# Attention of a hybrid encoder layer: four head groups written out, with the next group's queries placed bank by bank

## The reference

```python
q = (rms_norm(q_lat, q_a_norm) @ w_q_b)         # 512 latent -> 16 heads x (128 + 64)
kv = (rms_norm(kv_lat, kv_a_norm) @ w_kv_b)     # 512 latent -> 16 heads x (128 keys + 128 values)
s = (einsum(q_nope, k_nope) + einsum(q_rope, k_rope)) * scale
s = where(mask, s, -inf)                        # chunk-causal: a query sees keys up to its chunk of 64
o = einsum(softmax(s), v)
y_mla = (o * silu(gate)) @ w_o                  # 2048 x 2048
y_lru = (h * silu(gate)) @ w_o                  # 2048 x 2048, h from the recurrence
merged = sigmoid(m_mla) * y_mla + sigmoid(m_lru) * y_lru
```

## Time and profile before

| what | value |
|---|---|
| median of 3 runs | 2043.49 us |
| profiled execution | 2044.64 us, span 2042.8 us |
| PE busy | 1993.4 us, 98% of the span |
| DVE, ACT, POOL busy | 682.3, 716.8, 905.2 us (33%, 35%, 44%) |
| stretch of the attention's heads and projections | 1070 to 1321 us |
| mean granted TensorE clock | 0.996 of full speed |

### The profile page before, as it was taken

The page is one execution under the profiler, slowest core; times in us unless marked ns, Lnnn a source line. Parts: engine busy times, 40 slices in busy tenths (PEclk is TensorE's granted clock), DMA queues, the critical chain, the costliest instruction groups (busy, mean ns, idle before and its releaser), DMA issues.

```text
span 2042.8 us, 25478 instructions
## 1 busy us (share of the span) xinstructions
PE 1993.4 (98%) x9070; PEld 1658.4 (81%) x9070; DVE 682.3 (33%) x943; ACT 716.8 (35%) x1241; POOL 905.2 (44%) x683
## 2 busy tenths in 40 slices
PE   7999999999999999999999999899999999999996
PEld 6888888888888888888888878788888888888885
DVE  4100000000455647363456545781010250111344
ACT  6322232222353434433344444422222222333333
POOL 2444444444454545454452332154444454444452
PEclk9999999999999999999999999999999999999998
DMA  6533333433223323342352421343333343224232
GB/s 246 178 122 104 123 123 105 143 123 110 96 83 117 109 87 118 98 144 83 107 151 84 145 85 59 147 179 127 113 112 123 123 182 107 84 103 187 102 103 103
DMA packets 128688, 247.06 MB, mean 121 GB/s; under 512 B 15053, under 2 KB 40309, under 8 KB 120565
## 3 DMA queue, kind: packets, MB, share of 16 engines
q1 hardware_dynamic: 116688, 185.09, 27.7%
q10 hardware_dynamic: 11941, 61.17, 7.8%
HBM read 214.26 MB, written 29.36 MB: 119 GB/s over the span
## 4 chain that ended last, share of the span: by engine, by line
issue 59%; POOL 38%; POOLq 1%; DVE 1%; PE 0%; ACT 0%; DVEq 0%
POOL wlo L362 38%; POOLq L361 1%; POOLq L358 0%; DVE x L1241 0%; PE ps L1252 0%; DVE x L1214 0%; DVE stage L1213 0%; DVE x L1244 0%; POOLq L362 0%; ACT stage L790 0%; DVEq L126 0%; DVE nrm L827 0%; DVE nrm L832 0%; DVE nrm L833 0%; DVE nrm L828 0%
## 5 line engine op out<-in xcount | busy, mean ns | idle before, releaser
L362 POOL TENSOR_TENSOR wlo<-raw,whi 128x512 fp32r<-128x512 f32 x672 | 903.9, 1348 | 1111.9 <-ACT whi L378 1111.4
L378 ACT ACTIVATE whi<-raw 128x512 fp32r<-128x512 f32 x672 | 422.2, 632 | 1200.4 <-PE ps L1252 1153.1
L1252 PE MATMUL ps<-hhi,whi 128*128 128x512 f32 x1408 | 548.2, 389 | 1.2 <-POOL wlo L362 1.2
L1252 PE MATMUL ps<-hhi,wlo 128*128 128x512 f32 x1408 | 547.7, 389 | 0.0
L1252 PE MATMUL ps<-hlo,whi 128*128 128x512 f32 x1408 | 547.7, 389 | 0.0
L1252 PEld LDWEIGHTS ps<-hhi,whi 128*128 128x128 f32 x1408 | 264.4, 188 | 56.5 <-POOL wlo L362 1.6
L1252 PEld LDWEIGHTS ps<-hlo,whi 128*128 128x128 f32 x1408 | 264.4, 188 | 55.1 <-issue 0.2
L1252 PEld LDWEIGHTS ps<-hhi,wlo 128*128 128x128 f32 x1408 | 264.3, 188 | 54.7
L912 DVE TENSOR_TENSOR stage<-ps,stage 128x512 f32<-128x512 f32 x16 | 11.1, 692 | 412.4 <-ACT stage L475 410.9
L1252 PE MATMUL ps<-lhi,whi 128*128 128x512 f32 x256 | 100.4, 392 | 2.5 <-DVE llo L821 2.5
L1252 PE MATMUL ps<-llo,whi 128*128 128x512 f32 x256 | 100.3, 392 | 0.0
(11 more groups left out here) (253 smaller groups left out, 2420.0 us busy)
## 6 DMA issues: line engine op xcount, KB each, us to landing
raw<-in_w_in SPq DMA_DIRECT2D x88, 1024.0 KB, 5.0
raw<-in_w_o_lru SPq DMA_DIRECT2D x16, 1024.0 KB, 4.9
raw<-in_w_o_mla SPq DMA_DIRECT2D x16, 1024.0 KB, 4.9
raw<-in_w_out SPq DMA_DIRECT2D x16, 1024.0 KB, 5.0
raw<-in_w_ple_gate SPq DMA_DIRECT2D x16, 1024.0 KB, 4.9
sig_scr<-stage ACTq DMA_DIRECT2D x8, 1024.0 KB, 7.0
raw<-in_w_kv_b SPq DMA_DIRECT2D x32, 256.0 KB, 4.0
stage<-sig_scr ACTq DMA_DIRECT2D x8, 1024.0 KB, 4.8
```

The lines of the kernel that those rows point to most:

```text
L362: pool.tensor_tensor(wlo[:, k % RING], raw[:, k // RAWC, k % RAWC], whi[:, k % RING].bitcast(F32), ALU.subtract).then_inc(lo_ready, 1)
L378: act.activation(whi[:, c % RING], raw[:, c // RAWC % 2, c % RAWC], ACT.Copy).then_inc(hi_ready, 1)
L1252: return pe.matmul(o, l, r, start=start, stop=stop)
```

## The change

The loops over pairs of groups go on PE, ACT and DVE; the four groups are written out. In a group:

- Values are projected by token tiles (banks): tiles 0 and 1 for all four chunks, then tile 2, then the scores 3 and 2 of head 0, then tile 3 (12 matmuls), then the scores 1 and 0. A semaphore `v_done` counts tiles, so ACT and DVE take each from PSUM by itself.
- At the group's end stand the query chunks of the next group, or, in the last group, the first four chunks of the output projection of the recurrence's branch: bank 3 for all four chunks ahead of `values(2)`, bank 2 between the turns of head 3, banks 1 and 0 after them, then `values(3)`.
- ACT splits these four chunks into `whi` after the exps of heads 1, 2 and 3 (one, one, two).
- The next group's keys start with banks 0 to 2 of the first chunk ahead of the claim of the set.
- In the last group DVE splits `llo` tiles 0 to 3 inside heads 1 and 2, two in each; the others follow the attention.

```diff
+            def next_chunk(g, k, ms):
+                c = C_ATT + 3 * KL * (g + 1) + k
+                if ms == (3,):
+                    pe.wait_ge(lo_ready, c + 1)
+                for m in ms:
+                    hi, lo, kn = ahead(g, k, m)      # queries, or lhi/llo after wait_ge(l_split, k + 1)
+                    ...
+                if ms[-1] == 0:
+                    ins.then_inc(chunk_used, 1)
...
+                for m in range(3):
+                    keys(m)
+                if g:
+                    take(ks)
+                keys(3).then_inc(chunk_used, 1)
...
+                for k in range(KL):
+                    new_values(k, 0)
+                    new_values(k, 1)
+                for k in range(KL):
+                    new_values(k, 2)
+                take(ks)
+                pe.wait_ge(kr_lo, 2)
+                pe.wait_ge(qr_lo, g + 1)
+                scores(0, 3)
+                scores(0, 2)
+                for k in range(KL):
+                    new_values(k, 3).then_inc(chunk_used, 1)
+                scores(0, 1)
+                scores(0, 0)
+                for h in range(1, 4):
+                    scores(h, 3)
+                    scores(h, 2)
+                    if h > 1:
+                        values(h - 2)
+                    if h == 1:
+                        take(pt)
+                    for q in (3, 2, 1, 0):
+                        turn(h - 1, q)
+                    scores(h, 1)
+                    scores(h, 0)
+                pe.wait_ge(exp_done, 16 * g + 13)
+                for k in range(KL):
+                    next_chunk(g, k, (3,))
+                values(2)
+                turn(3, 3)
+                turn(3, 2)
+                pe.wait_ge(exp_done, 16 * g + 14)
+                for k in range(KL):
+                    next_chunk(g, k, (2,))
+                turn(3, 1)
+                turn(3, 0)
+                take(ks)
+                for k in range(KL):
+                    next_chunk(g, k, (1, 0))
+                values(3)
```

ACT, in a group's heads:

```diff
+                    if h < 4:
+                        exp(h, 2)
+                        exp(h, 1)
+                        exp(h, 0)
+                        split(c + 2 * KL + RING + h - 1)
+                    if h == 3:
+                        split(c + 2 * KL + RING + 3)
+                        act.wait_ge(exp_done, 16 * g + 16)
+                        act.sem_inc(released[ks], 1)
+                for k in range(KL):
+                    split(c + 3 * KL + RING + k)
```

DVE, in the heads:

```diff
+                        maximum(g, h, 1)
+                        maximum(g, h, 0)
+                    if h < 3 and g == NG - 1:
+                        split_merge(lhi, llo, l_split, 2 * h - 2)
+                        split_merge(lhi, llo, l_split, 2 * h - 1)
```

More of the change, by code:

```diff
@@ L647, in _ @@
             merge_gate_out(1, 0, U_M3, stage_idle)
[L649 to L723, removed]
@@ L728, in _ @@
                 act.dma_start(olo[:, 4 * g:4 * g + 4].bitcast(F32), o_scr[g]).then_inc(o_landed[g], 16)
-            with act.Fori(0, NG) as i:
-                for g in range(2):
+            merge_gate_back(0, 0)
+            for k in range(6, KD):
+                split(C_Y + RING + k)
+            with act.Fori(0, NG - 1) as i:
+                for g in (1, 2):
                     for k in range(KD):
@@ L733, in _ @@
                         if k == 2:
-                            act.wait_ge(y_out, i * 2 + (g + 1))
-                            act.dma_start(stage[:], sig_scr[bass.ds(i + (1 - g) * NG, 1)].rearrange("a q m n -> q (a m) n")).then_inc(sig_landed, 16)
+                            merge_gate_back(i + g // 2, g % 2)
+            for k in range(KD):
+                split(C_Y + RING + (2 * NG - 1) * KD + k)
+                if k == 2:
+                    merge_gate_back(NG - 1, 1)
             def x1_turned(g):
@@ L1130, in _, with maximum @@
-            step.leave(NG // 2)
-            signal(y_out)
-            for half, (hi, lo, done) in enumerate(((lhi, llo, l_split), (ohi, olo, o_split))):
-                for t in range(KD):
-                    if half == 0 and t == 0:
-                        dve.wait_ge(l_landed, 32)
-                    if half and t % 4 == 0:
-                        dve.wait_ge(o_landed[t // 4], 16)
-                    whole = lo[:, t].bitcast(F32)
-                    step(dve.tensor_copy(hi[:, t], whole))
-                    lo_of(lo[:, t], whole, hi[:, t]).then_inc(done, 1)
+            def maximum(g, h, q):
+                dve.wait_ge(s_done, 16 * g + 4 * h + (3 - q) + 1)
+                dve.reduce_max(snb[:, h % 2, q:q + 1], ps[:, 4 * (g % 2) + q, 0:(q + 1) * P], AX_X,
+                               negate=True).then_inc(nb_ready, 1)
@@ new lines, in projection_lo @@
+            def projection_lo(g, part, ms):
+                hi, lo = ((qnhi, qnlo), (knhi, knlo), (vhi, vlo))[part]
+                s = (part + g + 1) % 2
+                for m in ms:
+                    dve.wait_ge(proj_hi, 12 * g + 4 * part + m + 1)
+                    step(dve.scalar_tensor_tensor(lo[:, m], ps[:, 4 * s + m], 1.0 if part else SCALE,
+                                                  hi[:, m].bitcast(F32), ALU.mult, ALU.subtract), wait=m == 3)
+                    if m == 3:
+                        signal(released[s])
@@ L1144, in merge_lru @@
+            signal(y_out)
+            for t in range(KL, KD):
+                if t == 2 * KL:
+                    dve.wait_ge(l_landed, 32)
+                split_merge(lhi, llo, l_split, t)
+            for t in range(KD):
+                if t % 4 == 0:
+                    dve.wait_ge(o_landed[t // 4], 16)
+                split_merge(ohi, olo, o_split, t)
             def merge_lru(i):
@@ L1406, in _ @@
                     square_sum(4, 2)
-            with pe.Fori(0, NG // 2) as i:
-                use = list(U_ATT)
-                def take(s):
-                    claim(s, use[s], i, 5)
-                    use[s] += 1
-                def queries(b, ks):
-                    for k in ks:
-                        chunk(C_ATT + 12 * b + k, features, 1 - b, qlhi[:, k], qllo[:, k], k, KL, i, 24)
-                for b in range(2):
-                    ks, pt = b, 1 - b
-                    c = C_ATT + 12 * b
-                    if b == 0:
-                        take(pt)
-                        queries(0, range(KL))
+            use = list(U_ATT)
@@ new lines, in _, with keys @@
+            take(1)
+            for k in range(KL):
+                chunk(C_ATT + k, features, 1, qlhi[:, k], qllo[:, k], k, KL)
+            for g in range(NG):
+                ks, pt = g % 2, 1 - g % 2
+                c = C_ATT + 3 * KL * g
+                def keys(m):
+                    o = ps[:, 4 * ks + m]
+                    h, l = whi[:, c % RING, m * P:(m + 1) * P], wlo[:, c % RING, m * P:(m + 1) * P]
+                    mm(o, h, kvhi[:, 0], True, False)
+                    mm(o, h, kvlo[:, 0], False, False)
+                    return mm(o, l, kvhi[:, 0], False, False)
+                if g == 0:
@@ L1479, in _ @@
-                    for h in range(5):
-                        if h < 4:
-                            scores(h, 3)
-                            scores(h, 2)
-                        if h > 1:
-                            values(h - 2)
-                        if h == 1:
-                            take(pt)
-                        if h:
-                            turn(h - 1, 3)
-                            turn(h - 1, 2)
-                        if h == 4 and b == 0:
-                            take(ks)
-                            queries(1, range(2))
-                        if h:
-                            turn(h - 1, 1)
-                            turn(h - 1, 0)
-                        if h < 4:
-                            scores(h, 1)
-                            scores(h, 0)
@@ L1501, in _ @@
-                    if b == 0:
-                        queries(1, range(2, KL))
-                    values(3)
-            with pe.Fori(0, NG) as i:
-                for g, (hi, lo, done) in enumerate(((lhi, llo, l_split), (ohi, olo, o_split))):
-                    claim(1 - g, U_Y[1 - g], i, 1)
-                    for k in range(KD):
-                        pe.wait_ge(done, k + 1)
-                        chunk(C_Y + g * KD + k, features, 1 - g, hi[:, k], lo[:, k], k, KD, i, 2 * KD)
+                pe.wait_ge(lo_ready, c + KL + 1)
@@ L1514, in _, with attention_output @@
+            def attention_output(i):
+                claim(0, U_Y[0], i, 1)
+                for k in range(KD):
+                    pe.wait_ge(o_split, k + 1)
+                    chunk(C_Y + KD + k, features, 0, ohi[:, k], olo[:, k], k, KD, i, 2 * KD)
+            lru_output(0, KL, claimed=True)
+            with pe.Fori(0, NG - 1) as i:
+                attention_output(i)
+                lru_output(i + 1, 0)
+            attention_output(NG - 1)
             use = list(U_O)
```

308 lines of the change are left out of this document (196 added, 112 removed).

## The result

| kernel | median | runs | profiled span | granted clock |
|---|---|---|---|---|
| before | 2043.81 us | 10 | 2042.8 us | 0.996 |
| changed | 2049.40 us | 10 | 2048.4 us | 0.991 |

The ratio is 1.0024, with a 95% interval from 1.0016 to 1.0032: slower by 5.6 us. I had said 2047.5, with 2040 to 2053, and gave "slower" 0.48. The span grows by the same 5.6 us.

What follows compares the result with a forecast made beforehand. TensorE (PE) bounds the kernel, so only its waits or half clock give time back. Losses after, 19.6 + 3.7 + 2.7 + 0.5 + 3.6 = 30.1 us against 26.1 before, gave +4.0 and 2047.5 us, range 2040 to 2053.

Steps and rivals of the forecast that it cites:

- Starvation at chunks 2 and 3: At each group's end PE waits for chunks split only after head 3's last exp: 4.9 us per group, 19.6 in four.
- P: The end of head 3's last scores on PE, 1114.95 in group 0; the last exp was put at P + 3.5.
- First-head waits gone: Twelve value matmuls between head 0's scores cover exp and normalisation of the first head: 8.4 us gone but for 0.5.
- Values of heads 2 and 3, keys: PE waits of 1.26 us, 2.36 and 1.07 at these places all go, covered by the next query chunks.
- First output chunk: After the last group's attention, the 2.8 us wait does not go, as chunk 4's parts come late from DVE; 2.7 remain.
- Merge splits in the last group's heads: Four new DVE splits in heads 1 and 2 of group 3 make PE lose 1.7 and 2.0 us, sum 3.7.
- The clock: Three falls to half clock behind waits without matmuls, 1.2 us each, 3.6 us; bounds 0 and 8.
- the bound: Limit between same and slower: about 0.2%, 4.1 us, from no change; above 2047.6 us counts as slower.
- Rival C: Slower: clock falls after all four long stalls, at the output chunk and in last heads; +5 us, 2052 to 2053; chance 0.18.
- Rival B: Faster: last exps come 4.3 us earlier, so no wait at chunk 2; 2025, a half of it 2037; chance 0.12 with half.
- Rival D: An operand with small margin (query low parts 0.5, normalised rows 0.3) comes late: +4 us, 2051.5; chance 0.08.

Runs made afterwards that it cites:

- e1_splits_early: Changed kernel with ACT's splits of the next four chunks moved: 0 and 1 after head 1's exps, 2 and 3 after head 2's; 2024.53 us.
- e3_stall_filled: Changed kernel with 16 unused matmuls of 512 columns added between chunk 1 and chunk 2 of each group; 2044.84 us.
- e7_no_cover: Against the kernel with both moves (e5_both): all value matmuls stand ahead of the first scores again; 2022.41 us.
- e8_keys_claimed: Against e5_both: PE claims the bank set before the first keys of groups 1 to 3, not after banks 0 to 2; 2024.99 us.
- e2_chunks_later: Changed kernel with PE's order alone changed: chunks 2 and 3 for bank 3 after the turns of tiles 3 and 2 of head 3; 2032.95 us.
- e4_dve_before_keys: Changed kernel with DVE's four merge splits in the last group moved from heads 1 and 2 to before the keys' low parts; 2043.02 us.
- e5_both: Changed kernel with the moves of e1_splits_early and e4_dve_before_keys together; 2019.60 us.
- e9_values_whole: Against e7_no_cover: ACT takes no value tile from PSUM before all four chunks are done; 2026.28 us.

## Why the prediction was right, and where it was off

*Starvation at chunks 2 and 3*: right, in its place, its cause and its size. I had 4.25 us for chunk 2 and 0.65 for chunk 3; the trace has 4.08 and, in one group of four, 0.44. Moving the splits on ACT or the demand on PE takes it away, each by the amount the walk gives. The last exp ended at P + 3.5, as before; the copy of chunk 2 starts 0.10 us ahead of the end of its record (1115.34 and 1115.44), which is most of the difference.

*First-head waits gone*: right in that they go, with nothing left of the 0.5 I had kept. They were 9.1 to 9.2 us by starts, where I had 8.4; for example, the ten transposes with the wait in them took 1.74 us in group 0 (1098.55 to 1100.29) instead of 1.0, 0.73 lost where I took idle time plus 0.17. But I had put it all down to the twelve matmuls as cover, and that was wrong: without them only 0.47 us per group come back. The largest share that the runs show is the tile by tile hand-over, 1.0 us.

*Values of heads 2 and 3, keys*: gone, as forecast; the keys by a measured 1.00 us each against 1.07.

*First output chunk*: 2.34 left, I had 2.7.

*Merge splits in the last group's heads*: 3.2 us of DVE per head against 3.1, with one meeting with POOL, though it was the subtraction that met it and not the CAST. The first wait was 2.14 instead of 1.7. The second was 0.46 in the changed kernel instead of 2.0: the clock had fallen, so PE came later itself. In the runs in which it stood at full rate there it was 2.0.

*The clock* is the term that was mis-sized: I had counted three falls at 1.2 us for 3.6 us; there were six at 1.6 to 2.9, 12.4 us in sum. My bound of 8 for six or seven was too low as well. The waits were smaller than I had them by 5 us (21.5 against 26.5), part of it because slow matmuls fill later waits. That leaves the losses after 3.8 us above my 30.1; the losses before were about 0.8 above my 26.1, and 1.1 us fell away ahead of the attention, which I had not in the sum. So what is left between forecast and result, 1.9 us, is small because errors of 9 and 7 us went against each other, and that is luck. That the stall outweighs the covers is not: the experiments show it. The result lies on the slower side of the bound, which I had left open. Rival C named this, falls at nearly every long wait. The evidence I leaned on against it, the one pattern of group 1 that did not fall, was one of two, with half the idle time; that was too little to call three of seven. The windows agree with the rule of the Trainium skill ("TensorE: Matmul & The Clock Gate", section "Why this matters for your kernels") that a long idle gap between bursts of matmuls puts the array back to half rate: all four stalls of about 4 us were followed by the lower level, at 1.2 GHz, and the same stretch filled with idle work was not. But the clock also fell behind gaps of half that length, 1.98 us in the earlier trace rows, 1.95 and 2.18 here, so half the length was not on the safe side in this kernel.

*Rival B* would have needed the last exp 4.3 us earlier; it came no earlier than before. *Rival D*: neither of the two operands with the small margins came late; PE's wait table has no wait on them in first heads.

## What to carry to other kernels

When work is moved up to cover a wait, follow its own operands back through every engine's written order: here four chunks were moved up on PE, and two of them stayed behind the last exp on ACT. In a kernel whose PE is 98% busy a stall can cost more than its length (here 4.1 us and 1.7 to 2.9 behind it), since the matmuls behind it may run at half clock; count that for every stall longer than those which the trace already shows followed by a fall. And test which part of a combined change brings a gain before crediting the obvious one.

## What was unexpected of the hardware

The clock's fall is not tied to one wait. After the same 2.2 us of idle time at the free output chunk it fell in the profiles of the changed kernel, e1_splits_early, e3_stall_filled, e7_no_cover and e8_keys_claimed, and not in those of e2_chunks_later, e4_dve_before_keys, e5_both and e9_values_whole. In all eleven profiles of these kernels PE stood idle for 1.8 to 2.6 us eighteen times between 1050 and 1345 us, and eleven of these were followed by the lower level; all eight of 3.8 to 3.9 us were (changed kernel and e4_dve_before_keys). So kernels with the same waits differ by 1.6 us from one profile to another. Ahead of the attention, where the ten kernels other than the one before are the same, the first keys matmul starts between 1068.4 and 1070.4 us. Differences of that size between single profiles here are not worth an explanation.

A DVE subtraction that started just after POOL's (1299.57 against 1299.49) took 1.74 us instead of 0.69, as in the kernel before a CAST took 1.52 instead of 0.42: the DVE operation lost 1.05 to 1.1 us each time. In the changed kernel POOL's took 1.27 us, its usual time, so POOL's own record gave no sign of the meeting. In the kernel before it took 1.79 us, and in e4_dve_before_keys the three that met DVE took 1.50, 1.59 and 1.37.
